# Read-back gates of a PEER block: multiplied into the GELU results eight chunks at a time in the first table, or chunk by chunk in the second

## The reference, cut to what matters

```
q = (xf @ wq).reshape(t, PEER_HEADS, 2, PEER_HALF)      # scores, two top-16 lists, top-16 of their sums
gate = jax.nn.softmax(top, axis=-1)                     # (256, 8, 16)
u = jnp.take(u_tab, ib, axis=0)                         # rows of the first table, 16384 x 2048
act = jax.nn.gelu(jnp.einsum("thkd,td->thk", u, xb), approximate=False)
v = jnp.take(v_tab, ib, axis=0)                         # rows of the second table, 16384 x 2048
out = jnp.einsum("thk,thkd->td", gb * act, v)
```

## Time and profile before

| | us |
|---|---|
| median of 3 runs | 1837.03 |
| lowest, highest | 1830.07, 1838.16 |
| the profiled execution | 1842.05 |
| its span in the trace | 1840.3 |
| first table, about | 452 to 1187 |
| second table, about | 1189 to 1821 |
| mean granted TensorE clock | 0.99 |

### The profile page before, as it was taken

One profiled execution on the slowest core, in us unless ns is written; L12 is line 12 of the kernel. 1 busy time (PEld: TensorE's weight loads), 2 busy tenths in 40 slices (PEclk: granted clock), 3 DMA queues, 4 the chain that ended last, 5 costly groups with the idle time before them and its releaser, 6 DMA issues.

```text
span 1840.3 us, 34226 instructions
## 1 busy us (share of the span) xinstructions
PE 1771.6 (96%) x12247; PEld 1605.1 (87%) x12247; DVE 1282.2 (70%) x2166; ACT 874.5 (48%) x1434; POOL 521.6 (28%) x336
## 2 busy tenths in 40 slices
PE   7999979999999999999999999999999999999998
PEld 7998869999999999999999999977667777767776
DVE  7787676766989888444444444478888888878885
ACT  6545734444444444444444444455445545455554
POOL 0000000000007788777870000067721122112100
PEclk9999989999999999999999999999999999999999
DMA  7554538776557778777777555599999999999994
GB/s 252 204 189 138 175 91 252 229 244 217 191 188 189 188 189 189 189 188 189 189 188 257 188 188 188 196 307 334 358 342 348 359 359 351 338 363 348 347 322 127
DMA packets 188326, 445.62 MB, mean 242 GB/s; under 512 B 61153, under 2 KB 96241, under 8 KB 179697
## 3 DMA queue, kind: packets, MB, share of 16 engines
q1 hardware_dynamic: 148768, 373.48, 60.8%
q0 software_dynamic: 39504, 71.55, 14.5%
HBM read 423.79 MB, written 20.57 MB: 241 GB/s over the span
## 4 chain that ended last, share of the span: by engine, by line
PE 67%; DMA 15%; DVE 8%; issue 5%; ACT 4%; SPq 0%; DVEq 0%; ACTq 0%
PE ps L1435 19%; PE ps L1436 18%; PE ps L1437 18%; DMA raw<-v_tab 12%; DVE low L821 4%; DMA side<-gate_scratch 4%; ACT high L553 3%; PE ps L1665 2%; PE ps L1679 2%; PE ps L1681 2%; PE ps L1667 2%; PE ps L1677 2%; DVE big L1357 1%; DVE w_full L1366 0%; DVE big L831 0%
## 5 line engine op out<-in xcount | busy, mean ns | idle before, releaser
L821 DVE TENSOR_TENSOR low<-raw,high 128x1024 fp32r<-128x1024 f32 x638 | 769.5, 1222 | 420.3 <-ACT high L553 416.1
L1435 PE MATMUL ps<-act_hi,high 128*128 128x256 f32 x3056 | 871.3, 285 | 24.9 <-DVE act_lo L854 13.1
L1436 PE MATMUL ps<-act_lo,high 128*128 128x256 f32 x3056 | 866.5, 284 | 0.0
L1437 PE MATMUL ps<-act_hi,low 128*128 128x256 f32 x3056 | 866.3, 283 | 0.0
L553 ACT ACTIVATE high<-raw 128x1024 fp32r<-128x1024 f32 x638 | 657.4, 1058 | 278.4 <-DMA raw<-v_tab 162.3
L1435 PEld LDWEIGHTS ps<-act_hi,high 128*128 128x128 f32 x3056 | 588.2, 192 | 28.9 <-issue 17.1
L1436 PEld LDWEIGHTS ps<-act_lo,high 128*128 128x128 f32 x3056 | 588.4, 193 | 0.1
L1437 PEld LDWEIGHTS ps<-act_hi,low 128*128 128x128 f32 x3056 | 588.3, 192 | 0.0
L745 ACT ACTIVATE big<-ps 128x192 f32<-128x192 f32 x128 | 42.3, 330 | 423.2 <-PE ps L1437 423.2
L497 POOL DMA_INDIRECT gate_scratch<-gates_sb,cells_sb x128 | 213.2, 1666 | 66.2 <-issue 66.2
L517 POOL DMA_INDIRECT big<-v_tab,half_sb x64 | 99.7, 1558 | 362.5 <-DVE big L1357 358.8
(11 more groups left out here) (214 smaller groups left out, 1501.9 us busy)
## 6 DMA issues: line engine op xcount, KB each, us to landing
raw<-u_tab SPq DMA_DIRECT2D x256, 512.0 KB, 3.2
raw<-v_tab SPq DMA_DIRECT2D x256, 512.0 KB, 6.1
raw<-w_in SPq DMA_DIRECT2D x62, 512.0 KB, 3.8
raw<-w_out SPq DMA_DIRECT2D x32, 512.0 KB, 4.7
raw<-w_q SPq DMA_DIRECT2D x32, 512.0 KB, 4.6
gate_scratch<-side SPq DMA_DIRECT2D x32, 384.0 KB, 6.2
side<-gate_scratch SPq DMA_DIRECT2D x128, 96.0 KB, 6.1
act_scratch<-side SPq DMA_DIRECT2D x32, 128.0 KB, 5.2
```

Of the source, the lines that this page charges most:

```text
L821: V.tensor_tensor(slot(low, s), slot(raw, s), slot(high, s).bitcast(F32), ALU.subtract).then_inc(lo_done, 1)
L1435: mm(acc, wh, a_hi, start=(kk == 0), stop=False)
L1436: mm(acc, wh, a_lo, start=False, stop=False)
L1437: ins = mm(acc, wl, a_hi, start=False, stop=(kk == KT - 1))
```

## The change

The gates are read back in 16 groups of 8 chunks (786 KB each) into four buffers, which take the place of the row buffers of the units in `big`. SP issues group g behind the loads of chunk 97 + 2g of the first table. DVE multiplies a whole group of 1536 columns in place into the GELU results, between the two low parts of chunk 98 + 2g (groups 0 to 14), the last group behind the weights of expert 1 of the second table. `w_full` and `w_ok` are gone: ACT rounds the weights from `big`, and those of expert 0 before the last GELU. The semaphore `gated` counts the groups. The cell indices are computed behind chunk 72, not 120. POOL gathers rows 0 and 1 after group 15 of 16, and row 2 after the last group and the first 16 cells. PE's wait for the last GELU stands behind the first narrow matmuls. SP's loop over the second table is unrolled.

```
-FIRST_UNIT, LAST_UNIT = 9, 121
+FIRST_UNIT, LAST_UNIT = 8, 121
+GATE_CHUNKS = 8
+GATE_GROUPS = N_KEYS // GATE_CHUNKS
+GATE_BUFS = 4
+GATE_LOADS = N_KEYS - 1 - 2 * (GATE_GROUPS - 1)
...
-        gate_in = [side[:, 1024 + k * DENSE:1024 + (k + 1) * DENSE] for k in range(2)]
+        GATE_COLS = GATE_CHUNKS * DENSE
+        gate_in = [view(GELUS + k * GATE_COLS, GATE_COLS) for k in range(GATE_BUFS)]
...
+            def load_gates(g):
+                if g == 0:
+                    for r in range(ROUTE_STEPS):
+                        sp.wait_ge(scattered[r], 16 * TOPK if r % TB == 0 else 16 * SLOTS_HALF)
+                if g >= GATE_BUFS:
+                    sp.wait_ge(gated, g - GATE_BUFS + 1)
+                src = gate_scratch[GATE_CHUNKS * g:GATE_CHUNKS * (g + 1)].rearrange("r c t -> c r t")
+                dst = gate_in[g % GATE_BUFS].rearrange("p (r t) -> p r t", t=DENSE)
+                sp.dma_start(dst, src).then_inc(gate_back[g % GATE_BUFS], 16)
+
             for e in range(N_KEYS):
                 load(C_U + e, (C_U + e) % 2, u_tab[e])
                 if e % EXPORT == 0 and e >= 2 * EXPORT:
                     save_act(e // EXPORT - 2)
-            def gate_load(e, par):
-                sp.dma_start(gate_in[par], gate_scratch[e]).then_inc(gate_back[par], 16)
+                if e >= GATE_LOADS and (e - GATE_LOADS) % 2 == 0:
+                    load_gates((e - GATE_LOADS) // 2)
...
+            for e in range(2):
+                load(C_V_TAB + e, (C_V_TAB + e) % 2, v_tab[e])
             save_act(N_KEYS // EXPORT - 2)
-            for r in range(ROUTE_STEPS):
-                sp.wait_ge(scattered[r], 16 * TOPK if r % TB == 0 else 16 * SLOTS_HALF)
-            for j in range(2):
-                gate_load(j, (C_V_TAB + j) % 2)
+            load(C_V_TAB + 2, C_V_TAB % 2, v_tab[2])
+            save_act(N_KEYS // EXPORT - 1)
             sp.wait_ge(used, 2 * C_V_TAB)
-            save_act(N_KEYS // EXPORT - 1)
-            def second_table(first, end):
-                with sp.Fori(first, end) as i:
-                    for j in range(2):
-                        par = (C_V_TAB + j) % 2
-                        load(C_V_TAB + 2 + 2 * i + j, par, v_tab[2 * i + j + 2])
-                        sp.wait_ge(w_ok, 2 * i + j + 1)
-                        gate_load(2 * i + j + 2, par)
+            for e in range(3, N_KEYS):
+                load(C_V_TAB + e, (C_V_TAB + e) % 2, v_tab[e])
...
-            for n in range(ROWS):
+            pool.wait_ge(gated, GATE_GROUPS - 1)
+            for n in range(ROWS - 1):
                 gather_row(n)
             pool.wait_ge(cell_ok, 1)
             pool.wait_ge(act_saved, 16 * (N_KEYS // EXPORT))
             for n in range(per):
                 gather_cell(n)
+            pool.wait_ge(gated, GATE_GROUPS)
+            gather_row(ROWS - 1)
...
-            expert_steps(done, N_KEYS)
             def round_w(e, par):
-                act.wait_ge(w_ok, e + 1)
...
-                nc.scalar.activation(w_t[par][:, W_HI], w_full[:, :], ACT.Copy)
-                nc.scalar.activation(w_t[par][:, W_HI2], w_full[:, B_TOK], ACT.Copy).then_inc(wh_ok, 1)
+                nc.scalar.activation(w_t[par][:, W_HI], big[:, ds(e * DENSE, DENSE)], ACT.Copy)
+                nc.scalar.activation(w_t[par][:, W_HI2], big[:, ds(e * DENSE, SPARSE)], ACT.Copy).then_inc(wh_ok, 1)
+            expert_steps(done, N_KEYS - 1)
+            act.wait_ge(gated, GATE_GROUPS - 1)
             round_w(0, C_V_TAB % 2)
+            expert_step(N_KEYS - 1)
...
-            with act.Fori(0, N_KEYS // 2 - 3) as i:
+            for e in range(1, 5):
+                v_step(e, (C_V_TAB + e) % 2)
+            act.wait_ge(gated, GATE_GROUPS)
+            with act.Fori(0, N_KEYS // 2 - 5) as i:
...
+            def gate_group(g):
+                dve.wait_ge(gate_back[g % GATE_BUFS], 16 * (g // GATE_BUFS + 1))
+                dve.wait_ge(taken, C_U + GATE_CHUNKS * (g + 1))
+                part = view(g * GATE_COLS, GATE_COLS)
+                V.tensor_tensor(part, part, gate_in[g % GATE_BUFS], ALU.mult).then_inc(gated, 1)
...
-            cut_pairs(ROUTE_CHUNKS + 4, N_KEYS - 8)
+            cut_pairs(ROUTE_CHUNKS + 4, N_KEYS - 56)
             dve.wait_ge(swapped, 32 * ROUTE_BATCHES)
             V.tensor_scalar(unit_cols(cell_ix[:, :]), half_ix[:, :, 0, SLOTS_HALF:], float(SPARSE), route_sc[:, 2:3],
                             ALU.mult, ALU.add).then_inc(cell_ok, 1)
-            cut_pairs(N_KEYS - 8, N_KEYS)
+            for e in range(N_KEYS - 55, N_KEYS + 1):
+                cut_low_piece(C_U + e, (C_U + e) % 2, 0)
+                if e - 1 >= GATE_LOADS and (e - 1 - GATE_LOADS) % 2 == 0 and e < N_KEYS:
+                    gate_group((e - 1 - GATE_LOADS) // 2)
+                cut_low_piece(C_U + e, (C_U + e) % 2, 1)
...
-            def weights(e, par, between):
-                dve.wait_ge(gate_back[par], 16 * (e // 2 + 1))
-                dve.wait_ge(taken, C_U + 1 + e)
-                if e:
-                    dve.wait_ge(wl_ok, e)
-                V.tensor_tensor(w_full[:, :], view(e * DENSE, DENSE), gate_in[par], ALU.mult).then_inc(w_ok, 1)
-                between()
+            def weights(e, par):
                 dve.wait_ge(wh_ok, e + 1)
-                V.tensor_tensor(w_t[par][:, W_LO], w_full[:, :], w_t[par][:, W_HI].bitcast(F32), ALU.subtract).then_inc(wl_ok, 1)
+                V.tensor_tensor(w_t[par][:, W_LO], view(e * DENSE, DENSE), w_t[par][:, W_HI].bitcast(F32),
+                                ALU.subtract).then_inc(wl_ok, 1)
...
-                cut_low_piece(C_V_TAB + e, par, 0)
-                weights(e, par, lambda: cut_low_piece(C_V_TAB + e, par, 1))
+                cut_low(C_V_TAB + e, par)
+                weights(e, par)
+                if e == 1:
+                    gate_group(GATE_GROUPS - 1)
...
-            pe.wait_ge(taken, C_V_TAB)
...
                     narrow_rows(par, hf, start=start)
+                    if start and hf == 0:
+                        pe.wait_ge(taken, C_V_TAB)
                     wide_rows(par, hf, start=start).then_inc(used, 1)
```

More of the change, by code:

```diff
@@ L149, in build @@
         cell_ix = sb(ctx, "cell_ix", UNITS, U32)
-        w_full = sb(ctx, "w_full", DENSE)
         route_sc = sb(ctx, "route_sc", 8)
@@ L234, in build @@
         act_out = [side[:, k * EXPORT * SPARSE:(k + 1) * EXPORT * SPARSE] for k in range(2)]
-        gate_in = [side[:, 1024 + k * DENSE:1024 + (k + 1) * DENSE] for k in range(2)]
+        GATE_COLS = GATE_CHUNKS * DENSE
+        gate_in = [view(GELUS + k * GATE_COLS, GATE_COLS) for k in range(GATE_BUFS)]
+        assert GATE_BUFS * GATE_COLS <= ROWS * D
         assert SMALL + DENSE <= 1536
@@ L334, in build @@
         low_out = sem("low_out")
-        gate_back = [sem(f"gate_back{k}") for k in range(2)]
-        w_ok = sem("w_ok")
+        gate_back = [sem(f"gate_back{k}") for k in range(GATE_BUFS)]
+        gated = sem("gated")
         wh_ok = sem("wh_ok")
@@ L457, in _ @@
-            for q in range(H_PARTS + 2):
-                second_table(q, q + 1)
-                if q < H_PARTS:
-                    n = KT * DENSE // H_PARTS
[L461 to L465, removed]
+            for e in range(3, N_KEYS):
+                load(C_V_TAB + e, (C_V_TAB + e) % 2, v_tab[e])
+                if e - 3 < H_PARTS:
+                    n = KT * DENSE // H_PARTS
+                    a, b = (e - 3) * n, (e - 2) * n
+                    sp.dma_start(h_back[:, a:b], h_scratch[:, a:b]).then_inc(h_in, 16)
+                elif e - 3 < H_PARTS + 2:
+                    a = (e - 3 - H_PARTS) * D // 2
+                    sp.dma_start(g_last[:, a:a + D // 2], g_f[:, a:a + D // 2]).then_inc(gf_in, 16)
@@ L784, in v_step @@
                 round_w(e, par)
-            with act.Fori(0, N_KEYS // 2 - 3) as i:
+            for e in range(1, 5):
+                v_step(e, (C_V_TAB + e) % 2)
+            act.wait_ge(gated, GATE_GROUPS)
+            with act.Fori(0, N_KEYS // 2 - 5) as i:
                 for j in range(2):
-                    v_step(1 + 2 * i + j, (C_V_TAB + 1 + j) % 2)
+                    v_step(5 + 2 * i + j, (C_V_TAB + 1 + j) % 2)
             for e in range(N_KEYS - 5, N_KEYS):
@@ L1358, in sparse_unit @@
                                        op0=ALU.mult, op1=ALU.add).then_inc(row_used, 1)
-            def weights(e, par, between):
-                dve.wait_ge(gate_back[par], 16 * (e // 2 + 1))
-                dve.wait_ge(taken, C_U + 1 + e)
-                if e:
-                    dve.wait_ge(wl_ok, e)
-                V.tensor_tensor(w_full[:, :], view(e * DENSE, DENSE), gate_in[par], ALU.mult).then_inc(w_ok, 1)
-                between()
+            def weights(e, par):
                 dve.wait_ge(wh_ok, e + 1)
-                V.tensor_tensor(w_t[par][:, W_LO], w_full[:, :], w_t[par][:, W_HI].bitcast(F32), ALU.subtract).then_inc(wl_ok, 1)
-            weights(0, C_V_TAB % 2, lambda: None)
```

(3 more changed lines are left out.)

1 line of the change is left out of this document (removed).

## The result

The changed kernel takes 1823.88 us (median; 1821.33 to 1824.1) against 1836.0 us for the kernel before, measured beside it: a ratio of 0.9936, with a 95% interval of 0.9911 to 0.9961. It is 12 us faster, where the forecast was 32: the sign was right, the size 2.6 times too large. The 1824 us lie in the range, on the figure of rival 2.

The account below looks back on a forecast made before the run. It took the second table's middle as transfer-bound at 347 GB/s; -32.4 for gate reads, +2 for late pieces, -1.5 for the turn gave about -32 us, so 1805 us from 1837.03; range 1793 to 1826.

Parts of the forecast that it names:

- rival 2: Second table: the ring of load buffers, not the transfer rate, is the bound; 1823 us, chance 0.20.
- the first: Middle of second table: transfer-bound, so removing 11.01 MB of gate reads at 347 GB/s saves 32.4 us.
- the cycle of 9.9 us: Second table: a slot's landing 6.3, high part 1.06, low part 1.22 and unit share 1.34 us; 4.96 us an expert.
- 30.4: Middle of second table: forecast gain, 32.4 us from gate reads leaving, less 2 us estimated for late pieces.
- the turn: Between the two tables: PE no longer waits for the last GELU and the weights made after it; gain 1.5 us.
- the packets' time of the gate reads: Middle of second table: lower price of the reads, from the engine time left beside the pieces; only 13 us back.
- Reads in the first table, nothing: First table: sixteen 786 KB gate reads raise DMA share from 0.58 to 0.78, 257 GB/s, and cost nothing.
- rival 3: First table: gate reads landing later than 18 us hold DVE, making the kernel slower; 1846 us, chance 0.05.
- The last swap: First table, behind chunk 72: DVE waits for POOL's last swap before computing cell indices; PE loses 0 to 1.5 us, taken as 0.
- Row gathers, nothing: Near 1175 us: two row gathers meet the first second-table pieces; 0 to 2 us, taken as 0.
- the mutual waits, not counted: Second table: ACT no longer waits for DVE's product, nor DVE for a gate; nothing counted besides the bytes.
- The bandwidth rule: Middle of second table: HBM share of about 358 GB/s a core bounds traffic; remaining bytes would need 508.5 us.

Follow-up runs that it names:

- the deep kernels: Changed kernel (gate reads put back, unused) and kernel before, each with a third pair of load buffers and two cell gathers a unit: 1799.15 and 1802.1 us.
- a_wait: Changed kernel with a DVE copy of the weights put back between the low parts, for which ACT waits: 1823.03 us, ratio 0.9932.
- a_plus_reads: Changed kernel with a 96 KB gate read for each expert from 3 on put back into the second table, unused: 1824.48 us, ratio 0.9951.
- a_small_units: Changed kernel with DVE's operation of each unit cut from 2048 to 64 columns, same bytes loaded: 1810.77 us, ratio 0.9879.
- a_deep_ring: Changed kernel with a third pair of load buffers for the second table and ACT's loop over experts written out: 1811.98 us, ratio 0.9876.

## Why the prediction was right in sign and 2.6 times too large

**The step that failed** is the first: "What is left is 182.05 MB; at the same 347 GB/s that takes 524.6 us instead of 557", and ahead of it "the middle of the second table is bound by transfers". The kernel's own traffic of before, and later of the deep kernels, ran at 379 to 382 GB/s as soon as there were slots to load into. 347 GB/s was what four slots ask for, a result and not a cause. That a busy share of 0.95 means a full resource was the error; the share went to 1.01 under the same engines. Two lines of the prediction already spoke against it: single slices of 396 GB/s, and the cycle of 9.9 us, or 4.96 an expert, worked out for rival 2, which met the measured pace where the rate left it unexplained.

In its place: the middle won 19 us between the two traces, not 30.4, and the whole 12 us between the medians. No part owns them: the gate reads 3 to 6, the loop of SP 3 to 7, the turn 1.5, DVE's product 0 to 2; each but the turn is of the size of its own uncertainty, and how the 12 us divide stays open. The units, which begin one expert earlier, were not tested alone.

**Rival 2** had the mechanism, and its 1823 us are the measured time, but the figure met it partly by luck: it rested on 13 us for the packets' time of the gate reads, which measured 3 to 6, and it left the loop out. Its sum of 4.96 us an expert met the pace of before partly by chance as well: with the changed kernel's landing of 6.8 us in place of 6.3 the same sum gives 5.2 us an expert (an estimate), where 4.80 was measured, and taking 0.15 us out of the cycle brought a third of what the sum says. The runs show that the number of slots and the time of a unit set the pace; they don't show that the terms can be priced by adding them up.

**Reads in the first table, nothing:** right. Share 0.79 for a predicted 0.78, 251 GB/s for 257. The view of their line gives the landing:

```profile
DMA to landing us min/median/max: 6.7/7.5/8.2
```

That is far from the 18 us at which rival 3 began. DVE around one product of a group:

```profile
1105.17 1.23 DVE L829 TENSOR_TENSOR low<-raw,high 128x1024 fp32r<-128x1024 f32 x1 [3.40 <-ACT high L558]
1106.31 1.75 DVE L1351 TENSOR_TENSOR big<-big 128x1536 f32<-128x1536 f32 x1
1107.98 1.22 DVE L829 TENSOR_TENSOR low<-raw,high 128x1024 fp32r<-128x1024 f32 x1
```

1.75 us for a predicted 1.76, the second half late by as much, and PE without a gap over the whole stretch.

**The last swap, 0 to 1.5 us, taken as 0:** right, with little to spare. DVE stood 5.43 us for it, and had the next low part under way at 871.2:

```profile
871.04 0.25 DVE L1355 TENSOR_SCALAR cell_ix<-half_sb,route_sc 128x64 uint32<-128x64 uint32 x1 [5.43 <-DMA half_sb<-swap_sb]
871.21 2.35 DVE L829 TENSOR_TENSOR low<-raw,high 128x1024 fp32r<-128x1024 f32 x2
```

This execution runs 2.5 us behind that of before here, so the first half ends at 872.4 and PE needs it at 870.6 + 2.5 = 873.1: 0.7 us to spare. PE's window from 556 to 966 us shows 410.00 busy.

**The turn, 1.5 us:** right. PE goes from one table to the other without a gap, ahead of the last GELU:

```profile
1189.83 0.28 PE L1454 MATMUL ps<-act_hi,low 128*128 128x256 f32 x1
...
1189.94 0.63 PE L1681 MATMUL ps<-high,w_even 128*128 128x512 f32 x2
...
1190.37 0.22 ACT L754 ACTIVATE side<-ps 128x64 f32<-128x64 f32 x1
```

**Row gathers, nothing, and the mutual waits, not counted:** right in this execution, where PE is full from 1190 to 1228 us, and a_wait shows the second. In the traces of a_plus_reads and a_small_units PE stood for 7 and 8 us between 1214 and 1231 us; what made the pieces or the weights late there isn't shown.

**The bandwidth rule** (the Trainium skill, DMA: Bandwidth & Descriptors, section Bandwidth: about 358 GB/s for a core) doesn't bind here: 382 GB/s were measured over 100 us. Another page of the Trainium skill, Perfetto Trace Analysis, section Roofline, says that 358 is the share when both cores of a pair draw on the memory, and that one core alone can pull more, up to about 435. These runs agree with that one, as far as they go. With it in hand, 0.95 of the time busy at 347 GB/s would have been a question and not an answer.

## What to carry to other kernels

A queue that looks full is not yet the bound: multiply out the buffer cycle first (landing, every engine that must pass over the slot, whatever stands in their way, and the issue of the next load), and if that alone comes near the pace seen, the bytes may buy little and one more buffer much. Take the sum as a pointer to a test, not as a price: here two of its terms, tried alone, moved the time by about a third of what it says. The test is cheap and runs both ways: put the removed traffic back, and lengthen the ring; here the first cost 3 to 6 us and the second gave 11, or 22 with the next limit cleared too. When a fast path is cleared, look at the engine that feeds it (here POOL's gathers), and count the issuing engine's own delay wherever it closes a cycle.

## What the runs showed of the hardware that was not expected

- The sixteen DMA engines of the core carried 379 and 380 GB/s over 400 us, with a share of 1.01 in the profile; the share of 0.95 to 0.96 in the kernel before hid at least 8% more throughput (352 against 380 in nearly the same stretch).
- In SP's loop a load was issued 0.17 to 0.18 us after the end of the low part that it waits for, written out 0.03 us after it.
- The packets' time of a queue is no price. In the first table a piece took 1.56 us of the engines; priced by what was left over, the gate reads came to 13 us, and measured 3 to 6.
- A few us without work lowered PE's granted clock beyond the gap itself: 0.66 in the 10 us around the 3.03 us stall of a_deep_ring, 0.83 to 0.86 in 10 to 12 us around each of four stalls of 2.1 to 3.0 us in the kernel before.
